# Down projection of 12 of 22 hidden tiles by seven products in three passes, with the root of the mean square multiplied into those tiles

## What is computed

```
def swiglu(h, w_gate, w_up, w_down):
    return (jax.nn.silu(h @ w_gate) * (h @ w_up)) @ w_down
...
    for layer in range(DEPTH):
        g = norm_gains[layer]
        h = h + 0.5 * swiglu(rmsnorm(h, g[0]), ffn_w_gate[layer, 0], ffn_w_up[layer, 0], ffn_w_down[layer, 0])
        ...
        h = h + 0.5 * swiglu(rmsnorm(h, g[2]), ffn_w_gate[layer, 1], ffn_w_up[layer, 1], ffn_w_down[layer, 1])
```

## Time and profile before

| | us |
|---|---|
| median of 3 runs | 1823.25 (1822.76 to 1823.81) |
| profiled execution, from first to last instruction | 1821.0 |
| PE busy in it | 1801.7 (99%) |
| DVE busy | 1344.8 (74%) |
| ACT busy | 859.6 (47%) |
| POOL busy | 53.1 (3%) |
| DMA | 176.87 MB, mean 97 GB/s |

### The profile page before, as it was taken

The page is one execution under the profiler, slowest core; times in us unless marked ns, Lnnn a source line. Parts: engine busy times, 40 slices in busy tenths (PEclk is TensorE's granted clock), DMA queues, the critical chain, the costliest instruction groups (busy, mean ns, idle before and its releaser), DMA issues.

```text
span 1821.0 us, 32718 instructions
## 1 busy us (share of the span) xinstructions
PE 1801.7 (99%) x13456; PEld 1720.7 (94%) x13456; DVE 1344.8 (74%) x1814; ACT 859.6 (47%) x1404; POOL 53.1 (3%) x68
## 2 busy tenths in 40 slices
PE   8999999999999999999999999999999999999997
PEld 8999999999999999999999999999998899889986
DVE  7766887557778966896798578855656799568954
ACT  8443464335446543554555335534423565335542
POOL 0000000000000000000000000000124000000000
PEclk9999999999999999999999999999999999999999
DMA  5255233341222333233223322333312223332331
GB/s 179 85 96 116 95 115 108 102 135 59 70 70 82 101 99 108 89 105 105 82 93 108 97 98 97 107 112 112 93 59 70 70 82 105 102 106 93 111 111 57
DMA packets 81107, 176.87 MB, mean 97 GB/s; under 512 B 7292, under 2 KB 12700, under 8 KB 80960
## 3 DMA queue, kind: packets, MB, share of 16 engines
q1 hardware_dynamic: 80544, 174.49, 31.3%
q10 hardware_dynamic: 416, 0.29, 0.0%
HBM read 171.35 MB, written 3.41 MB: 96 GB/s over the span
## 4 chain that ended last, share of the span: by engine, by line
PE 96%; DVE 2%; ACT 1%; DMA 0%; SPq 0%; issue 0%; DVEq 0%; ACTq 0%
PE psum L2028 25%; PE psum L2098 13%; PE psum L2100 13%; PE psum L2101 13%; PE psum L2038 7%; PE psum L2037 4%; PE psum L2041 4%; PE psum L2036 4%; PE psum L2040 3%; PE psum L2148 2%; PE psum L2147 2%; PE psum L2149 2%; PE psum L2157 2%; DMA rb_sb<-in_rel_bias 0%; DVE rms L1391 0%; PE psum L2336 0%
## 5 line engine op out<-in xcount | busy, mean ns | idle before, releaser
L2098 PE MATMUL psum<-fh,wh 128*128 128x264 f32 (+1 forms) x1968 | 559.9, 285 | 2.2 <-ACT psum L728 2.2
L2101 PE MATMUL psum<-fh,wl 128*128 128x264 f32 (+1 forms) x1968 | 557.2, 283 | 0.0
L2100 PE MATMUL psum<-fl,wh 128*128 128x264 f32 (+1 forms) x1968 | 556.7, 283 | 0.0
L2098 PEld LDWEIGHTS psum<-fh,wh 128*128 128x128 f32 x1968 | 371.1, 189 | 3.5 <-issue 3.0
L2100 PEld LDWEIGHTS psum<-fl,wh 128*128 128x128 f32 x1968 | 370.9, 188 | 0.6
L2101 PEld LDWEIGHTS psum<-fh,wl 128*128 128x128 f32 x1968 | 369.8, 188 | 0.0
L588 ACT ACTIVATE wh<-raw 128x1024 fp32r<-128x1024 f32 (+2 forms) x194 | 169.2, 879 | 224.1 <-PE psum L2028 172.7
L2028 PE MATMUL psum<-xs,wh 128*128 128x264 f32 (+1 forms) x1504 | 267.3, 297 | 5.0 <-DVE xs L1341 3.5
L1226 DVE TENSOR_TENSOR wl<-raw,wh 128x1024 fp32r<-128x1024 f32 (+2 forms) x193 | 194.7, 1016 | 95.8 <-ACT wh L588 95.1
L2028 PEld LDWEIGHTS psum<-xs,wh 128*128 128x128 f32 x1504 | 213.7, 189 | 15.6 <-issue 5.2
L2038 PE MATMUL psum<-hs,wh 128*128 128x512 f32 x528 | 206.6, 391 | 0.0
(11 more groups left out here) (314 smaller groups left out, 3000.4 us busy)
## 6 DMA issues: line engine op xcount, KB each, us to landing
raw<-in_w_gate_up SPq DMA_DIRECT2D x175, 512.0 KB, 3.7
raw<-in_w_down SPq DMA_DIRECT2D x64, 384.0 KB, 3.2
raw<-in_w_down SPq DMA_DIRECT2D x64, 320.0 KB, 3.0
raw<-in_od_in SPq DMA_DIRECT2D x21, 512.0 KB, 3.5
raw<-in_ev_in SPq DMA_DIRECT2D x18, 512.0 KB, 3.5
raw<-in_ev_out SPq DMA_DIRECT2D x8, 512.0 KB, 3.5
raw<-in_od_out SPq DMA_DIRECT2D x8, 512.0 KB, 3.5
x<-in_x_t SPq DMA_DIRECT2D x8, 264.0 KB, 4.9
```

What stands on the lines that cost most here:

```text
L2098: pe.matmul(psum[:, bank, 0:w], wh[:, slot, cols], high_x, start=start and j == 0, stop=False, skip_group_check=True)
L2100: pe.matmul(psum[:, bank, 0:w], wh[:, slot, cols], low_x, start=False, stop=False, skip_group_check=True)
L2101: last = pe.matmul(psum[:, bank, 0:w], wl[:, slot, cols], high_x, start=False, stop=j == 3, skip_group_check=True)
```

## The change

**Three passes.** The hidden tiles of a block are taken as 6, 6 and 10. For the first two passes (only the second in block 0, whose first pass stays plain) the down projection is made by seven products as well. A pass of 6 tiles has three up groups and then two down groups; a down group makes four output tiles (two upper, two lower) with 14 products of three tiles of contraction, so 9 matmuls of 264 columns each. The weight quarters of a down group are 2 x 384 columns wide. The last 10 tiles keep the plain down projection.

**Hidden tiles as inputs of products.** The down products need forms of the hidden tiles (differences of their halves), so the root and the factor 0.5 must be in the tiles already: `gate_a_root` and `gate_b_root` multiply `rms` into the gate once more, and `up_a_out` and `up_b_gate` carry the 0.5. Then `fold_first` and `fold_others` form the differences and `fold_a_lows`, `fold_b_lows` and their ACT counterparts split them. The output of a down group is added to `x` by `upper_rows` and `lower_rows`, one instruction for a row block, in place of the four of `down_residual`.

**Sums s3 and s1 by DMA.** `sum_s3` and `sum_s1` on DVE go away. The first operand is loaded by SP and the second is added to it by a DMA from POOL's queue with an accumulate (`accumulate_s3`, `accumulate_s1`). `raw` gets a fifth slot for s3.

**Fewer plain products.** In block 0 no `p2` is plain any more.

**Orders.** Each kind of group (entry, after entry, folding, turn, after turn, ...) has an order of its own on PE, DVE and ACT, written out. In a turn group, the first down group of a pass, products are cut: the first two tiles of contraction (`js=known`) run before the third (`js=rest`).

```diff
-PASS_F0 = (0, 10)
-PASS_F = (10, 12)
+PASS_F0 = (0, 6, 12)
+PASS_F = (6, 6, 10)
+TURNED = 2
...
+def form(g):
+
+    q, p, kind, _ = JOBS[g]
+    if enters(g):
+        return "entry" if q else "first_entry"
+    if leads(g):
+        return "turn"
+    if enters(g - 1):
+        return "after_entry" if q else "after_first_entry"
+    if leads(g - 1):
+        return "after_turn"
+    if ends(g):
+        return "last"
+    if is_down(g - 1):
+        return "up_after_down" if folds(g) else "straight_after_down"
+    return "folding" if folds(g) else "straight"
...
 def plain(g):
 
-    q, p = PASS_OF[g]
-    return p == 0 and g < GROUP[q, p][0] + 2
+    q = JOBS[g][0]
+    return q > 0 and not is_down(g) and g < ENTERED[q] + 2
...
+            def accumulate_s1(g):
+
+                slot = raw_slot("s1", g)
+                pool.wait_ge(raw_in[slot], RAW_COUNT["s1", g])
+                pool.dma_start(landing("s1", g), weights_of(JOBS[g][0], g, 1, 1), accum_op=ALU.add).then_inc(s1_added, 16)
...
+            def gate_a_root(g, real):
+                lo = N_META if real else 0
+                dve.wait_ge(silu_done, 2 * ups_before(g) + 1)
+                dve.tensor_tensor(gate[:, lo:L], gate[:, lo:L], rms[:, lo:L], ALU.mult).then_inc(dve_step, 1)
...
+            def upper_rows(n, real):
+
+                xm = halves(x[:, 2 * JOBS[n // 2][3] + n % 2, :], real)
+                dve.wait_ge(p3_done, n + 1)
+                dve.tensor_tensor(xm, rows_a(4 * (n % 2), real), xm, ALU.add).then_inc(a_out, 1)
...
+            def fold_a_lows(g, real):
+
+                j = JOBS[g][3]
+                dve.wait_ge(fold_high, 2 * turned_before(g) + 1)
+                dve.tensor_tensor(folded(B11, j, 1, real), halves(up, real)[:, 0, :], f32(folded(B11, j, 0, real)), ALU.subtract)
+                dve.tensor_tensor(folded(T1, j, 1, real), unfolded(T1, j, real), f32(folded(T1, j, 0, real)),
+                                  ALU.subtract).then_inc(fold_low, 1)
...
+            def turn_group(g, q, real):
+                n = 2 * g
+                gate_a_root(g - 1, real)
+                c22(n - 1, real)
+                sum_s4(g)
+                c21(n - 1, real)
+                gate_b_root(g - 1, real)
+                low_s1(g)
+                up_a_out(g - 1, real)
+                up_b_gate(g - 1, real)
+                fold_first(g - 1, real)
+                low_s4(g)
+                fold_a_lows(g - 1, real)
+                fold_others(g - 1, real)
+                low_a12(g)
+                fold_b_lows(g - 1, real)
...
+            def product(g, kind, s, x_form, bank, start, real, q=None, js=None):
+
+                w, count = width(real), reach(g)
...
+                for j in range(count) if js is None else js:
+                    if is_down(g):
+                        pe.wait_ge(fold_low, 2 * (turned_before(g) - count + j) + (1 if x_form in (B11, T1) else 2))
+                        high_x, low_x = folded(x_form, j, 0, real), folded(x_form, j, 1, real)
...
+            def turn_group(g, q, real):
+                n = 2 * g
+                known, rest = range(reach(g) - 1), (reach(g) - 1,)
+                p7(n, real, js=known)
+                p4(n - 1, real)
+                p3(n - 1, real)
+                p7(n + 1, real, js=known)
+                p5(n, real, js=known)
+                p1(n, real, js=known)
+                p1(n + 1, real, js=known)
+                p1(n, real, js=rest)
+                p1(n + 1, real, js=rest)
+                p5(n + 1, real, js=known)
+                p6(n, real, js=known)
+                p6(n + 1, real, js=known)
+                p2(n, real, js=known)
+                p7(n, real, js=rest)
...
+            def folding_group(g, q, real):
+                n = 2 * g
+                p7(n, real)
+                p1(n, real)
+                p3(n - 1, real)
+                p4(n - 1, real)
+                p6(n, real)
+                p7(n + 1, real)
+                p1(n + 1, real)
+                p5(n, real)
+                p6(n + 1, real)
+                p2(n, real)
+                p2(n + 1, real)
+                p3(n, real)
+                p4(n, real)
+                p5(n + 1, real)
```

More of the change, by code:

```diff
@@ new lines, in after_entry_group @@
+            def after_entry_group(g, q, real):
+                n = 2 * g
+                low_s1(g)
+                gate_a_root(g - 1, real)
+                sum_s4(g)
+                up_a_out(g - 1, real)
+                gate_b_root(g - 1, real)
+                low_s4(g)
+                fold_first(g - 1, real)
+                up_b_gate(g - 1, real)
+                fold_a_lows(g - 1, real)
+                fold_others(g - 1, real)
+                low_a22(g)
+                c22(n, real)
+                fold_b_lows(g - 1, real)
+                low_a11(g + 1)
+                c21(n, real)
+                gate_a_out(g, real)
+                gate_b_scale(g, real)
+                sum_s2(g + 1)
+                low_s3(g + 1)
+                low_s2(g + 1)
+                low_b21(q, real)
@@ new lines, in up_after_down_group @@
+            def up_after_down_group(g, q, real):
+                n = 2 * g
+                low_s1(g)
+                upper_rows(n - 1, real)
+                sum_s4(g)
+                c21(n - 1, real)
+                low_s4(g)
+                low_a12(g)
+                low_s3(g + 1)
+                c22(n, real)
+                low_a22(g)
+                gate_a_out(g, real)
+                low_a11(g + 1)
+                lower_rows(n - 1, real)
+                sum_s2(g + 1)
+                c21(n, real)
+                gate_b_scale(g, real)
+                low_s2(g + 1)
@@ L2041, in ffn_passes, with from_x @@
                 return pe.matmul(a, wl[:, slot, w], both[:, k, 0, 0:FRONT], start=False, stop=stop)
[L2043 removed]
+            def from_x(n, tile, v=None, real=False, first=False, between=None, wide=False, beside=False, both=late):
                 halved = first and n == 0
```

1642 lines of the change are left out of this document (1098 added, 544 removed).

## The result

The changed kernel takes 1861.11 us, median of 4 runs (1859.67 to 1872.5), where the kernel before takes 1823.17 on the same chip. The ratio is 1.022, 95% interval 1.020 to 1.024: 2.2% slower, where 1808.6 us was forecast and the range ended at 1828. The profiled execution has a span of 1857.7 us, 3.4 under the median of the runs.

The account below looks back on a forecast made before the run. PE's own work was taken as the bound. Span 1821.0 less 31.1 us on PE, plus 14 for turns and 2.5 for folding groups, gave 1806.4; 2.2 more for the runs' median made 1808.6 us, range 1793 to 1828.

Parts of the forecast that it names:

- PE's list: PE's work over the whole kernel: folded passes, fewer plain `p2` and four waits removed shorten it by 31.1 us.
- the sum: Whole kernel: span 1821.0 less 31.1 on PE, plus 14 for turns and 2.5 for folding groups, gives 1806.4 us.
- The turn: Entry to the down groups of a folded pass: PE loses 2.0 us at each of seven, 14 us, bounds 2 and 28.
- The 1.0 for the last third of `p1`: At a turn, PE loses 1.0 us as `p1`'s last third waits for `fold_a_lows` on DVE.
- the 0.4 for `low_s1`: At a turn, PE loses 0.4 us as `p5` waits for `low_s1` on DVE.
- the 0.6 for the second `p6`: At a turn, PE loses another 0.6 us as the copy for the second `p6` stands behind highs on ACT.
- 95% was reckoned: In a folding up group, DVE has 19.4 us of work against 20.4 of PE, 95% busy, so it fits.
- its rival: DVE runs behind through the folding groups if 33 instructions take 1.7 us longer; 1816 to 1828 us, chance 0.12.
- The folding groups: `p1_copy` comes late on ACT, costing PE 0.25 us in each of ten groups: 2.5 us, bounds 0 and 6.
- The accumulating DMA: Two in each of 55 groups, 6.4 to 7.4 us long, covered by 7.5 us or more, so costing nothing.
- third rival: The accumulate outlasts its cover and holds `sum_s2` on DVE, deciding from about 8.5 us; 1820 and far up, chance 0.17.
- With no new wait the span would be 1790: Whole kernel: span once PE's list is 31.1 us shorter; as a rival, 1792 to 1800 us, chance 0.18.

Follow-up runs that it names:

- e17: e10 with the 110 DMAs on POOL's queue writing without adding (output not the reference's); 1815.2 us.
- e3: e1 with the 110 DMAs on POOL's queue writing without adding (output not the reference's); 1821.3 us.
- e5: The changed kernel, table rows still in two bundles, with the 110 DMAs on POOL's queue writing without adding (output not the reference's); 1845.3 us.
- e9: The changed kernel with one table row ahead of each output tile's weight loads in the first down projection, and neither accumulate adding; 1825.4 us.
- e1: The changed kernel with block 0's eight table rows issued one a group in groups 3 to 10, not in two bundles of four; 1846.2 us.
- e13: e3 with the two multiplications by the root in a folding group cut to 8 of 528 columns; 1818.05 us.
- e12: The changed kernel with table rows issued early, one at each of the first stage's last four loads and the first down projection's first four tiles; 1834.1 us.
- e10: e12 with a sixth slot, so that every other group's s1 is loaded and summed a group ahead; 1826.5 us.
- e8: The changed kernel with one table row per tile of the first down projection, and s1's load and accumulate each cut into two halves; 1853.8 us.
- e14: The kernel before with only its table rows moved, four behind the weight loads of each of its first two groups; 1823.9 us.

## Why the prediction was wrong

- **PE's list.** "PE's list gets shorter by 31.1 us" holds. In block 1 the trace has 880 matmuls of the plain down projection before and 400 after, so 96 pairs fewer, and 504 product matmuls more. At 0.720 us a pair and 0.1215 a matmul that is 69.1 - 61.2 = 7.9 us, as predicted. What the sum left out is small: products start 0.1220 us apart in the changed kernel in block 1 and 0.1215 before, some 1.2 us in its 2304 matmuls. The pitch is the same in e17, so it is not the additions that stretch it.
- **The sum without disturbance.** e17, with early rows and no adding, is the nearest to the prediction's conditions. It is 8 us faster than before, where the sum says 14.6. By blocks it has 553.80, 351.23, 552.04 and 355.93 us, so -1.5, -2.9, -2.9 and -0.7. The rest is a wait of 1.8 us in the second group of block 0, waits in the groups of entry, 0.7 at the very end, and the pitch.
- **The turn.** Taken as 2.0 us in three waits. Measured at each of seven: 0.78 and 0.27 idle by the waits, 0.93 and 0.44 from start to start, 1.4 in all. The 1.0 for the last third of `p1` was right; the 0.4 for `low_s1` did not occur; of the 0.6 for the second `p6`, 0.44 did. The rows of PE at one turn:

```profile
659.90 0.36 PE L2735 MATMUL psum<-hf,wh 128*128 128x264 f32 x1 [0.78 <-DVE hf L1911]
662.60 0.36 PE L2735 MATMUL psum<-hf,wh 128*128 128x264 f32 x1 [0.27 <-issue]
```

  The term was 4 us too dear, which hid a little of the rest.
- **DVE.** It was busy for 54.36 of 59.90 us in the three up groups of a folded pass (the row at 690.50), 91% where 95% was reckoned, and its rival did not come true. That rival's "33 instructions" are 27 by the prediction's own list, so its 1.7 us would have been 1.35.
- **The folding groups.** 0.25 us in ten groups was taken; in blocks 1 and 2 the trace shows 0.2 each. Not in the sum were the groups behind each entry. PE loses 0.55, 0.8 and 1.2 us there in block 1 beyond the usual step, and 0.55, 0.85 and 2.0 in block 3. In e17 nothing above 0.4 is left in these places, so transfers made the most of it.
- **The accumulating DMA: the first step that failed.** Its length was forecast well, 6.4 to 7.4 us against a median of 6.2. The step that failed is "DMA traffic grows by some 77 MB on 177, far from filling engines that are busy a third of the time". The megabytes were nearly right (257.98 on 176.87, so 81), the conclusion was not. A group's own traffic goes from four quarters to seven, two of them with double packets. By the 0.30 of the earlier trace rows that is 0.30 x 9 / 4 = 0.68, and the trace has 0.71; without the additions it is 0.30 x 7 / 4 = 0.53, and e17 has 0.53. Plain loads of 512 KB take 4.8 us where the earlier trace rows had 3.7, single ones 7 and more, and a cover worked out from 3.7 and 7.4 does not hold. Most of that growth is the seven quarters and not the adding: with nothing added the median is 4.3 to 4.6 (e3, e5, e9, e17), and adding brings 0.2 to 0.5 more. e17, with a median of 4.6, came within 7 us of the sum, so longer plain loads by themselves cost little. This is the third rival's side, but not its mechanism: it decided on one long accumulate from 8.5 us on, at the turns. In the runs the price is spread, 14 to 25 us with one slot, and a single chain can be far over the median (10.9 us in e1).
- **The table rows: the step that was missing.** "With no new wait the span would be 1790" left out a part of the diff. Its eight DMAs move past SP's weight loads, from a place with cover to one without. They cost 27 us, most of it in two stalls of PE. The earlier trace rows had the warning, 8.6 us for 160 KB, and I used the row only as an upper bound for another DMA.
- **The range.** It ended at 1828, the upper end of a DVE that falls behind. e13 puts the share of the root on DVE at 3 us, so this rival was the wrong reserve. With a chance of 0.17 for "1820 and far up", but a range cut at 1828, the likely size of a transfer's mistake stood outside.

The two causes do not simply add up: the additions cost 15.8 us beside the bundles and 24.9 with a row in each group. The difference between e12 and e10, 7.5 us, is what a second place for s1 gives while both quarters are added; how much of it is cover for the additions and how much for the plain load of s1 is not told apart, as e12 was not run without adding. Which single late load costs which stall in blocks 1 to 3 is open.

## What to carry to other kernels

List every DMA that changes its place in a queue, small ones first, and ask which work hid it before and which hides it now: eight transfers of 160 KB cost 27 us between weights that were wanted at once, and next to nothing 90 us earlier. Price such a transfer by the time for which it fills the engines, and not by its bytes: a row of 160 KB took 6 us of them. Judge added traffic by the stretch in which it falls and by packets, not by megabytes over the whole span: four quarters at 0.30 become 0.7 with seven quarters, two of them added. Where loads run at such a share, cover has to be counted with the long ones of a chain, not with the medians of a quiet profile.

## What was not expected of the hardware

- An accumulating DMA moves twice the packets of a plain one and takes the engines twice as long: 29920 packets and 18.2% against 14944 and 9.4% for 54.01 MB (after, e3). Its own time to landing grows less, from 4.9 to 6.2 us for 512 KB.
- Accumulates of 256 KB land after 6.6 us, those of 512 KB beside them after 5.9 (e8).
- Four DMAs that each write one row of 1280 bytes 128 times to memory hold the issuing queue for 11 us: 0.6 us for each of the first two, 3.7 and 6.2 for the others. Issued one at a time between other loads, each holds it for 0.5 to 0.75 us (before, e1); with a single load between two of them it is up to 5.5 (e12).
- Such a row of 160 KB keeps the DMA engines 84% busy at 27 GB/s, and four land 6 us apart (after; 83% and 27 GB/s in e14).
- The granted clock falls to half (0.50) within a stall of PE of 18 us and within one of 11 us, and the matmuls behind them start 0.22 us apart, for 5.9 and 3.9 us. It happens behind a shorter stall too: in e1 PE waited 4.8 us, the clock was 0.50 from 313 to 318 us, and the matmuls there start 0.22 us apart.
